# Rotary row exchanges by transfers inside SBUF in place of permutation products, and two query heads rotated inside the attention

## The reference, cut to what matters

```python
def rotary(x, pos):                 # retention: q and k of each head, 64 wide
    x1, x2 = x[..., :half], x[..., half:]
    return concatenate([x1 * cos - x2 * sin, x2 * cos + x1 * sin], axis=-1)

def _rope_axis(x, ang):             # latent queries: halves of 8, for row and column
    x1, x2 = x[..., :half], x[..., half:]
    return concatenate([x1 * cos - x2 * sin, x2 * cos + x1 * sin], axis=-1)

q_mla = _mla_q(qn, _axial_rope(qr, ang_r, ang_c))   # 64 unrotated, 32 rotated
o_mla = _blocked_attention(q_mla, k_mla, v_mla)
```

## Time and profile before

| what | value |
|---|---|
| runs (us) | 2397.44, 2401.75, 2402.91; median 2401.75 |
| profiled execution | 2397.45 us, its span 2395.5 us |
| PE busy | 2325.3 us, 97% |
| POOL, DVE, ACT busy | 1102.9, 912.2, 874.8 us |
| PE's granted clock | 0.995 of full speed over the span |
| bytes moved | 231.37 MB, mean 97 GB/s |

### The profile page before, as it was taken

How to read it: one execution, slowest core, us unless ns; L and a number is a source line. 1 busy time by engine, 2 the same in 40 slices (tenths; PEclk the granted TensorE clock), 3 DMA queues, 4 the chain that set the end, 5 groups by cost and what they waited for, 6 DMA issues and landing times.

```text
span 2395.5 us, 33550 instructions
## 1 busy us (share of the span) xinstructions
PE 2325.3 (97%) x12124; PEld 1891.2 (79%) x12124; DVE 912.2 (38%) x1561; ACT 874.8 (37%) x1240; POOL 1102.9 (46%) x1356
## 2 busy tenths in 40 slices
PE   7999999899999999999999999999999999999997
PEld 6778687588888888888888888877766787888886
DVE  3324532498877771110111045234126554111113
ACT  3354543444233453212211234255434534422222
POOL 3333455099877764333333334333332054555544
PEclk9999999999999999999999999999999999999999
DMA  4222132256555531111211122222221022222222
GB/s 155 92 76 85 53 123 81 95 181 200 189 193 186 193 124 62 62 62 62 70 62 62 62 80 69 71 93 69 79 81 48 1 97 67 98 91 97 97 97 97
DMA packets 66604, 231.37 MB, mean 97 GB/s; under 512 B 7216, under 2 KB 9520, under 8 KB 66352
## 3 DMA queue, kind: packets, MB, share of 16 engines
q1 hardware_dynamic: 50656, 180.02, 21.9%
q10 hardware_dynamic: 15824, 49.55, 6.1%
HBM read 226.66 MB, written 2.10 MB: 95 GB/s over the span
## 4 chain that ended last, share of the span: by engine, by line
PE 60%; POOL 20%; issue 17%; DVE 2%; ACT 0%; POOLq 0%; DVEq 0%; ACTq 0%
PE ps L1783 46%; POOL WLO L343 20%; PE ps L2317 4%; PE ps L1818 1%; PE ps L2431 1%; PE ps L2444 1%; PE ps L2259 1%; PE ps L2288 1%; PE ps L2302 1%; PE ps L2432 1%; PE ps L2274 0%; PE ps L1804 0%; PE ps L1800 0%; PE ps L1799 0%; PE ps L2403 0%
## 5 line engine op out<-in xcount | busy, mean ns | idle before, releaser
L343 POOL TENSOR_TENSOR WLO<-RAW,WHI 128x256 fp32r<-128x256 f32 x1340 | 1087.5, 844 | 1248.7 <-ACT WHI L378 1248.0
L1783 PE MATMUL ps<-HLO,WHI 128*128 128x512 f32 (+2 forms) x1840 | 612.6, 367 | 5.7 <-DVE Y L1519 2.1
L1783 PE MATMUL ps<-HHI,WLO 128*128 128x512 f32 (+2 forms) x1840 | 605.3, 363 | 0.0
L1783 PE MATMUL ps<-HHI,WHI 128*128 128x512 f32 (+2 forms) x1840 | 604.2, 362 | 0.0
L378 ACT ACTIVATE WHI<-RAW 128x1024 fp32r<-128x1024 f32 x335 | 354.4, 1059 | 663.0 <-DMA RAW<-in_stream_dram 655.3
L1783 PEld LDWEIGHTS ps<-HLO,WHI 128*128 128x128 f32 (+1 forms) x1840 | 318.7, 188 | 69.0 <-issue 4.6
L1783 PEld LDWEIGHTS ps<-HHI,WHI 128*128 128x128 f32 (+1 forms) x1840 | 317.8, 188 | 58.9 <-issue 3.6
L1783 PEld LDWEIGHTS ps<-HHI,WLO 128*128 128x128 f32 (+1 forms) x1840 | 318.3, 188 | 55.8
L1378 DVE TENSOR_TENSOR SF<-SF,ps 128x512 f32<-128x512 f32 (+1 forms) x66 | 51.2, 777 | 495.5 <-PE ps L1783 486.3
L1783 PE MATMUL ps<-GLO,WHI 128*128 128x512 f32 (+1 forms) x704 | 231.6, 364 | 1.9 <-POOL WLO L343 1.9
L1783 PE MATMUL ps<-GHI,WLO 128*128 128x512 f32 (+1 forms) x704 | 231.5, 364 | 0.0
(11 more groups left out here) (373 smaller groups left out, 2887.9 us busy)
## 6 DMA issues: line engine op xcount, KB each, us to landing
RAW<-in_stream_dram SPq DMA_DIRECT2D x335, 512.0 KB, 3.2
ADA<-in_ada_dram ACTq DMA_DIRECT2D x72, 512.0 KB, 4.3
BM<-in_bias_dram ACTq DMA_DIRECT2D x8, 448.0 KB, 3.6
DECAY<-in_decay_dram ACTq DMA_DIRECT2D x4, 512.0 KB, 4.4
out_dram<-X SPq DMA_DIRECT2D x8, 256.0 KB, 2.2
X<-in_x_dram SPq DMA_DIRECT2D x2, 512.0 KB, 5.6
X<-in_x_dram ACTq DMA_DIRECT2D x2, 512.0 KB, 6.6
C<-in_mem_dram ACTq DMA_DIRECT2D x1, 1024.0 KB, 5.6
```

Of the source, the lines that this page charges most:

```text
L343: op = nc.gpsimd.tensor_tensor(WLO[:, slot(u), k:k + 2], RAW[:, slot(u), k:k + 2], WHI[:, slot(u), k:k + 2].bitcast(F32), ALU.subtract)
L1783: mm = nc.tensor.matmul(out, w, x[:, k, tok], start=(k == 0 and n == 0), stop=(k == kt - 1 and n == 2))
```

## The change

ret_swap moves from PE to ACT: behind the copy of QF (and of KF) ACT waits for its own copy and issues four transfers of 32 rows each into new tiles QS and KS; before the next copy of QF it waits until the last turn's transfers have landed. For the latent queries ACT waits for its own copy and, from head 2, for the rope of head h-2, and issues four transfers of 8 rows each into a new tile MQS; these stand ahead of the two MK transfers. DVE reads QS, KS and MQS where it read PSUM banks. Heads 6 and 7 are rotated inside the attention, at n = 1 and n = 3. turn_query goes, with PE's waits on mq_rope in it and in mla_values. The exchange of the latent key (one product) stays.

```diff
 def ret_raw(i):                                   # ACT
     convert(RET_Q[i] + AHEAD)
     wait_unit(RET_Q[i])
+    if i:
+        act.wait_ge(s("ret_swap0"), 64 * i)
+        act.wait_ge(s("ret_swap1"), 64 * i)
     nc.scalar.activation(QF[:], ps[:, 5], ACT.Copy).then_inc(s("ret_f"), 1)
+    ret_swap(i, 0)
     convert(RET_K[i] + AHEAD)
     wait_unit(RET_K[i])
     nc.scalar.activation(KF[:], ps[:, 6], ACT.Copy).then_inc(s("ret_f"), 1)
+    ret_swap(i, 1)
+def ret_swap(i, a):                               # ACT
+    x, swapped = ((QF, QS), (KF, KS))[a]
+    act.wait_ge(s("ret_f"), 2 * i + a + 1)
+    if i:
+        act.wait_ge(s("ret_r"), 6 * i)
+    for r in range(0, P, 32):
+        act.dma_start(swapped[r:r + 32], x[r ^ 32:(r ^ 32) + 32]).then_inc(s(f"ret_swap{a}"), 16)
...
 for h in range(8):                                # ACT, latent queries
     nc.scalar.activation(q[0:QK_MLA, h % 4], ps[0:QK_MLA, UQ_BANKS[h % 4]], ACT.Copy).then_inc(s("mq_raw"), 1)
+    act.wait_ge(s("mq_raw"), h + 1)
+    if h >= 2:
+        act.wait_ge(s("mq_rope"), 3 * (h - 2) + 3)
+    for r in range(64, QK_MLA, 8):
+        act.dma_start(MQS[r:r + 8, h % 4], q[r ^ 8:(r ^ 8) + 8, h % 4]).then_inc(s(f"mq_swap{h % 2}"), 16)
...
-dve.wait_ge(s("ret_swap"), 2 * i + 1)             # DVE, ret_rope
-V.tensor_tensor(TN[:, 1], ps[:, 3], SIN[:], ALU.mult).then_inc(s("ret_r"), 1)
+dve.wait_ge(s("ret_swap0"), 64 * i + 64)
+V.tensor_tensor(TN[:, 1], QS[:], SIN[:], ALU.mult).then_inc(s("ret_r"), 1)
...
-                    if n == 1:                    # DVE, attend
-                        query_rope(7)
+                    if n in (1, 3):
+                        query_rope(6 + n // 2)
...
-            for h in range(7):
+            for h in range(6):
                 query_rope(h)
...
-            ret_swap(0)                           # PE
...
-                ret_swap(i + 1)
...
-                if h:
-                    turn_query(h - 1)
...
                 if n == 1:                        # PE, mla_scores
-                    turn_query(7)
+                    pe.wait_ge(s("mq_raw"), 8)
...
-                if j == 4:                        # PE, mla_values
-                    pe.wait_ge(s("mq_rope"), 24)
```

More of the change, by code:

```diff
@@ L98 @@
 CTX_SEMS = dict(sq=("ret_sq", 4), acc=("ret_n", 4), ms=("ret_ms", 4), ln=("ret_copy", 4), rs=("ret_rs", 8), t=("ret_t", 4),
-                x=("ret_sc", 8), hi=("ret_hi", 4), lo=("ret_lo", 4), y=("ret_f", 8), up=("ret_swap", 8))
+                x=("ret_sc", 8), hi=("ret_hi", 4), lo=("ret_lo", 4), y=("ret_f", 8), up=("ret_swap0", 256))
 NA_COUNTS = dict(s=16, m=32, e=32, t=32, at=32, x=64, r=32, o=16, hi=4, lo=4)
@@ L213, in build @@
         (MQB,), _ = region(c_at, ("MQB", [P, 4, S], F32))
+        (MQS,), _ = region(q_at + 4 * S * 15 + 2048, ("MQS", [P, 4, S], F32))
         (MOHI, MOLO, MP, MPT), _ = region(q_at - 6144, ("MOHI", [P, 4, S], F32R), ("MOLO", [P, 4, S], F32R),
@@ L1113, in ret_rope @@
                 V.scalar_tensor_tensor(KR[:], ps[:, 6], RET_DK ** -0.5, COS[:], ALU.mult, ALU.mult).then_inc(s("ret_r"), 1)
-                dve.wait_ge(s("ret_swap"), 2 * i + 1)
-                V.tensor_tensor(TN[:, 1], ps[:, 3], SIN[:], ALU.mult).then_inc(s("ret_r"), 1)
+                dve.wait_ge(s("ret_swap0"), 64 * i + 64)
+                V.tensor_tensor(TN[:, 1], QS[:], SIN[:], ALU.mult).then_inc(s("ret_r"), 1)
                 dve.wait_ge(s("ret_r"), 6 * i + 3)
                 V.tensor_tensor(QR[:], QR[:], TN[:, 1], ALU.add).then_inc(s("ret_r"), 1)
-                dve.wait_ge(s("ret_swap"), 2 * i + 2)
+                dve.wait_ge(s("ret_swap1"), 64 * i + 64)
                 dve.wait_ge(s("ret_r"), 6 * i + 4)
-                V.scalar_tensor_tensor(TN[:, 1], ps[:, 4], RET_DK ** -0.5, SIN[:], ALU.mult, ALU.mult).then_inc(s("ret_r"), 1)
+                V.scalar_tensor_tensor(TN[:, 1], KS[:], RET_DK ** -0.5, SIN[:], ALU.mult, ALU.mult).then_inc(s("ret_r"), 1)
                 dve.wait_ge(s("ret_r"), 6 * i + 5)
@@ L1712, in _, with rope @@
                 na_step(n)
[L1714 removed]
+            def rope(tag, x, turned, cos, sin, n):
                 r = slice(64, QK_MLA)
[L1717 removed]
+                V.tensor_tensor(turned[r], turned[r], sin[r], ALU.mult).then_inc(s(tag), 1)
                 V.tensor_tensor(x[r], x[r], cos[r], ALU.mult).then_inc(s(tag), 1)
                 dve.wait_ge(s(tag), n + 2)
[L1720 removed]
+                V.tensor_tensor(x[r], x[r], turned[r], ALU.add).then_inc(s(tag), 1)
             dve.wait_ge(s("mtab_landed"), 32)
             dve.wait_ge(s("kr_swap"), 1)
[L1724 removed]
+            rope("kr_rope", KR2[:, 0:S], ps[:, 6], COSK, SINK, 0)
             norm2("ckv", 2, [(lambda k: psf[:, 1024 * k:1024 * k + N2], 0, N2, lambda k: col("g_kv", k))], RSK, TNK, CVHI, CVLO)
@@ L1733, in query_rope @@
             def query_rope(h):
-                dve.wait_ge(s("mq_swap"), h + 1)
-                rope("mq_rope", (MQA if h < 4 else MQB)[:, h % 4], 4 + h % 4, COSQ, SINQ, 3 * h)
-            for h in range(7):
+                dve.wait_ge(s(f"mq_swap{h % 2}"), 64 * (h // 2) + 64)
+                rope("mq_rope", (MQA if h < 4 else MQB)[:, h % 4], MQS[:, h % 4], COSQ, SINQ, 3 * h)
+            for h in range(6):
                 query_rope(h)
@@ L1861, in ret_value @@
                             hi=HHI, lo=HLO)
-            def ret_swap(i):
-                pe.wait_ge(s("ret_f"), 2 * i + 1)
-                nc.tensor.matmul(ps[:, 3], const[:, SWAP64], QF[:], start=True, stop=True).then_inc(s("ret_swap"), 1)
-                pe.wait_ge(s("ret_f"), 2 * i + 2)
-                nc.tensor.matmul(ps[:, 4], const[:, SWAP64], KF[:], start=True, stop=True).then_inc(s("ret_swap"), 1)
             def ret_scores(i):
@@ L2405, in _ @@
                 mm.then_inc(units_done, 1)
-            def turn_query(h):
-                pe.wait_ge(s("mq_raw"), h + 1)
-                if h >= 4:
-                    pe.wait_ge(s("mq_rope"), 3 * (h - 4) + 3)
-                nc.tensor.matmul(ps[0:QK_MLA, 4 + h % 4], const[0:QK_MLA, SWAPM, 0:QK_MLA], (MQA if h < 4 else MQB)[0:QK_MLA, h % 4],
-                                 start=True, stop=True).then_inc(s("mq_swap"), 1)
             for h in range(8):
```

1 line of the change is left out of this document (added).

## The result

The changed kernel takes 2409.03 us in the median of six runs (2403.66 to 2410.07), the kernel before 2400.14 on the same chip (2395.51 to 2402.91): ratio 1.004 with a 95% interval of [1.003, 1.005]. It is slower by 8.9 us, where 5.9 of gain were forecast. The profiled execution of the changed kernel is the fastest of its six, 2403.66 us, with a span of 2401.7.

A forecast was written before the change was run, and what follows sets the result against it. TensorE's own work, busy 97% of the span, was taken as the bound. Retention 1.3 plus latent queries 4.8, less 0.1 and 0.1, gave 5.9 us gained: 2395.8 us from the median 2401.75, range 2390.5 to 2406.

The forecast's parts named there:

- I take 1.9: Both stages: I, the time of four transfer issues on ACT, taken as 1.9 us within 1.3 to 3.7.
- The ceiling: Both stages: the 16 products removed free 14.0 us of PE time, the most that could be gained.
- exchanged for a wait for SQ: Retention's last three turns: PE waits for ACT's square instead of running the 1.82 us of products; -0.45 us in all.
- the formula for ret_total: Retention's later turns: ret_total starts at 100.2 plus the time of four issues, 102.1, 0.15 us later than before.
- The schedule of ACT per head: Latent queries: ACT needs 4.8 us per head for heads 0 to 3, 3.6 for 4 to 7; PE's period is 4.14.
- The second head inside the attention: Latent attention: head 7's rope at n = 3, some 2.1 us of DVE, fits mostly into idle time and costs 0.1.
- rival (a): Both stages: every issue costs what MK's does, 2.4 us for four; gain only 1.1, 2400.6 us; chance 0.22.
- (d): Latent stage: ACT's stream becomes the bound at the first Exp behind 32 issues; slower, 2409 us at 3.2 per four; chance 0.15.
- the schedule's own table: Latent queries: gain at the first Exp by price of four issues, from 6.1 us at 1.36 to -8.6 at 3.7.
- the first turn's 1.7: Retention's first turn: PE goes straight to the second pair of value units, 1.7 us earlier, with 1.1 of cover.
- Rival (b): Latent stage: only the eight-row issues are dear, 2.4 us for four; gain 2.7, 2399.0 us; chance 0.08.
- (c): Latent stage: transfers land after 6 us instead of 4.3, delaying later issues; gain 2.6 in all, 2399.1 us; chance 0.08.

The follow-up runs named there:

- no_transfer: Changed kernel without its transfers, the rotations left out: 2387.98 us, ratio 0.9959 to the kernel before.
- one_issue: Changed kernel with one transfer, copying rows where they are, in place of each four, so the exchange is left out: 2391.79 us, ratio 0.9966 to the kernel before.
- sp_both: Changed kernel with all 64 exchange transfers issued by SyncE instead of ACT, in both stages: 2387.47 us, ratio 0.9952 to the kernel before.
- changed_again: The changed kernel unaltered, measured once more: 2406.29 us, ratio 1.0033 to the kernel before.
- lat_only: Changed kernel with retention taken back to its products, so only the latent queries are changed: 2400.27 us, ratio 1.0008 to the kernel before.
- fill_behind: Changed kernel with two constant products per retention turn added behind ret_total: 2411.26 us, ratio 1.0046 to the kernel before.
- ret_only: Changed kernel with the latent queries taken back to products, so only retention is changed: 2403.44 us, ratio 1.0018 to the kernel before.
- ret_halves: Retention part of the change alone, issued by ACT, with half of the gate unit's products put ahead of ret_total: 2390.01 us, ratio 0.9972 to the kernel before.
- fill: Changed kernel with constant products on PE where the turning products stood, in both stages: 2403.94 us, ratio 1.0021 to the kernel before.
- sp_ret: Retention part of the change alone, its transfers issued by SyncE, latent stage as before: 2394.43 us, ratio 0.9986 to the kernel before.
- sp_lat: Latent part of the change alone, its transfers issued by SyncE, retention with its products: 2392.13 us, ratio 0.9968 to the kernel before.
- sp_halves: Changed kernel, both stages' transfers issued by SyncE, half of retention's gate products ahead of ret_total: 2387.00 us, ratio 0.995 to the kernel before.

## Why the prediction was wrong

The paths were right; the step that failed first is the price of an issue, "I take 1.9", where four took 2.5 in retention and 2.65 in the latent stage. From the forecast gain of 5.9 to the traces' loss of 8.4 are 14.3 us. The price of the issues makes 6.9 of them (3 x 0.6 in retention, 4.8 to -0.3 in the latent stage), the lower clock, for which the prediction has no term, 4.0, the first turn's gain that didn't come 1.7, the DECAY issue 0.6; some 1.1 are left, most of it in the latent stage.

**Right.** The ceiling and how it is read; that retention's products would be "exchanged for a wait for SQ"; the formula for ret_total. It counts KF's copy, I, DECAY, copy and square, and for I = 1.9 it puts ret_total 17.75 us behind the scores (84.35 to 102.1). With the measured 2.50, and a DECAY issue of 0.60 in place of 0.4, it gives 17.75 + 0.6 + 0.2 = 18.55, and 18.57 were measured. The schedule of ACT per head too: 4.8 us with I = 1.9 is 5.5 with 2.65, measured 5.55. The idle time before the scores stayed 0.78. The second head inside the attention cost nothing to be seen where the clock stayed up: from the first Exp to the end no_transfer, one_issue and sp_both take 575.7 to 575.9 us, the kernel before 575.8.

**Wrong: the price of an issue.** "I take 1.9", and the reason, that the rows are of COSQ's length. Measured: 2.44 to 2.64 for four in retention, 2.61 to 3.24 in the latent stage. Of the rows at hand the transfer inside SBUF, MK's median of 0.60, was the right one; it has 32 rows, as retention's have, and the length of the rows decided nothing. That is rival (a), to which 0.22 was given, and at 2.65 in the latent stage its way to (d): the schedule's own table gives 1.6 of gain at 2.4 and -1.4 at 2.8, so -0.3 at 2.65. (The same numbers give a gain of nothing in both stages together at I = 2.5, not at the 2.6 that it names.) Measured were -1.45; 0.6 of what is missing is the very first of these issues (1.22 us where the others took 0.64), and some 0.3 a gap between the first and the second issue of head 3, whose cause isn't shown: the kernel has no wait there.

Two readings of the rows go with it. An issue was dearer right behind another: of the four at 68.2 the first took 0.52 and the others 0.61 each, and DECAY's load, which took 0.34 at 97.93 in the kernel before, took 0.60 behind the four here. And "ACT does nothing else while it issues" is too wide: that issue at 97.93 ran beside KF's copy (97.92, 0.60 long). The new issues stand behind a wait for their own copy, so for them it holds.

**Missing: what an idle PE costs beyond its length.** No step priced the clock. The 2.7 us before ret_total went with a lower clock in two turns of three, 1.6 and 1.5 us, and 0.9 more were lost behind the first Exp, where the clock was 0.74 over 1815 to 1835. That goes with the clock in other kernels too: from the first Exp to the end, changed, changed_again, lat_only and fill_behind take 576.7 to 577.6 us, and before, ret_only and ret_halves, which keep the latent stage and a clock of 1.00 there, 575.5 to 575.8. Without the clock the formulas with the right I would have given about -1, first turn included, and about -3 without its 1.7 and with the dearer DECAY; that is inside the range, and the 4.0 us of the clock put the kernel outside it. The forecast had 1.9 us of idle time in each turn and asked nothing about the clock.

**Wrong: the first turn's 1.7.** The scores began at 59.45 for 59.47. The unit's lows came late, as the timeline shows:

```profile
46.44 0.36 PE L1839 MATMUL ps<-WLO,HHI 128*128 128x256 f32 x1 [1.40 <-POOL WLO L345]
```

The cover of 1.1 us was read from an execution in which the unit before was converted at 36.27; here it was at 37.35 (its transfer landed later), and I was 0.55 longer. Without transfers the scores begin at 58.04, with them at 59.05 to 59.45 in the nine kernels that have transfers and no turning products there, one issue or four, ACT or SyncE. In five of the nine, the changed kernel among them, PE waits 1.0 to 1.4 us there for POOL; in no_transfer it doesn't. Whether the exchange's traffic beside the weights' is what makes the lows late isn't settled. One execution tells little here: lat_only, which is the kernel before up to there, began at 60.93, with a lower clock behind an earlier wait, of 2.3 us (a mean of 0.86 over 30 to 42 us, 1.00 in the kernel before).

**The rule weighed in the prediction** (the Trainium skill, DMA: Bandwidth & Descriptors, "Why a DMA increments its semaphore by 16 and not by 1") would make eight-row issues dearer. By the medians they are, 0.63 to 0.64 against 0.61 us: the trace agrees in sign, and four cost some 0.17 us more, 1.3 over the eight heads. That an extra write is the reason isn't shown. Rival (b) is out, since retention's issues were dear as well. So is (c): landing took 2.6 us in the median in retention, in the latent stage DVE began 2.0 to 3.5 us after the last issue's start, not 6, and one_issue shows that it costs nothing. Rival (d), slower by ACT's stream ahead of the first Exp, is what the latent stage did, in a smaller size than priced.

## What to carry to other kernels

Price a transfer by its issue, in the stream that issues it, and take that price from the row that is most like it in source, target, rows and what is issued just ahead of it; then look at what stands behind it in that stream. With the same products gone, the same 64 issues made this kernel 9 us slower on ScalarE and 12 to 13 us faster on SyncE. Before a product is taken from TensorE, look at what it covers: if the wait behind it becomes longer than it was, put other work of TensorE in its place, since idle time may cost more than its own length.

## What was not expected of the hardware

- An issue inside SBUF took 0.61 us with 32 rows and 0.63 to 0.64 with 8 rows on ACT's queue, 0.59 and 0.62 on SyncE's. As a single one it took 0.51 with 32 rows and 0.48 with 128 rows of the same length. The kernel's loads from DRAM of such rows took 0.33 and 0.45.
- Of the twelve idle stretches of 2.7 us before ret_total in changed, changed_again, ret_only and fill_behind, eight were followed by a stretch at the lower granted clock, 1.2 GHz, which cost 1.5 to 1.7 us of a turn. None of those of 0.8 us in fill and of 1.2 us in no_transfer, one_issue, sp_both and sp_ret was. In the latent attention all four of 2.7 us (changed, changed_again, lat_only, fill_behind) were, and so were one of 2.12 in fill, one of 1.77 in sp_lat and one of 1.47 in sp_ret, but not the 1.67 in the kernel before. And all fourteen traces have one wait of 2.2 to 2.4 us for POOL, at 33 us: in six (lat_only, fill, fill_behind, one_issue, sp_halves, sp_ret) the lower clock followed, a mean of 0.86 over 30 to 42 us, in the other eight it stayed at 1.00, changed, changed_again and ret_only among them. So the length alone doesn't decide; what else does was not tried.
- DVE's products with both operands in SBUF took longer beside POOL than the 0.95 that was read before:

```profile
1814.70 1.24 DVE L1738 TENSOR_TENSOR MQS<-MQS,SINQ 32x512 f32<-32x512 f32 x1 [4.44 <-DMA MQS<-MQB]
```

  So it was at each of the three heads whose operation began with POOL at work, 0.90 to 1.24 us; the other five, with POOL idle, took 0.68, as at 1827.15. It was not on the path that set the end.
